# RWKV-7 scan on one Trainium2 core: 64x64 products that change partition halves by a table, and PSUM banks by kind

## The reference

```python
def wkv7_scan(r, w, k, v, a, b, reverse):
    def step(S, inp):
        rt, wt, kt, vt, at, bt = inp
        sa = jnp.einsum('bhvk,bhk->bhv', S, at)
        S = S * wt[:, :, None, :] + sa[..., None] * bt[:, :, None, :] + vt[..., None] * kt[:, :, None, :]
        return S, jnp.einsum('bhvk,bhk->bhv', S, rt)
    _, y = lax.scan(step, jnp.zeros((Bn, H, N, N), jnp.float32), xs, reverse=reverse)
```

## Time and profile before

| | |
|---|---|
| median of 3 runs (lowest to highest) | 2111.11 us (2107.66 to 2114.34) |
| the profiled execution | 2115.72 us, of which 2113.9 us from the first to the last instruction |
| the scan's first product to its last | 680.7 to 1156.7 us, 476 us |
| PE, PEld busy over the span | 83%, 65% |
| DVE, ACT, POOL busy over the span | 52%, 40%, 13% |
| mean granted PE clock | 0.92 of full |

### The profile page before, as it was taken

One profiled execution on the slowest core, in us unless ns is written; L12 is line 12 of the kernel. 1 busy time (PEld: TensorE's weight loads), 2 busy tenths in 40 slices (PEclk: granted clock), 3 DMA queues, 4 the chain that ended last, 5 costly groups with the idle time before them and its releaser, 6 DMA issues. The chain is left out here.

```text
span 2113.9 us, 48310 instructions
## 1 busy us (share of the span) xinstructions
PE 1755.0 (83%) x20423; PEld 1365.2 (65%) x20423; DVE 1109.5 (52%) x1786; ACT 846.8 (40%) x1228; POOL 280.2 (13%) x371
## 2 busy tenths in 40 slices
PE   3999999759776898898988399229999999999980
PEld 3777777647354888888887277226766666666650
DVE  4458988154575333333323832435656656556546
ACT  4246665110142333333322221025655556556532
POOL 0010000000110423333222200040000000000003
PEclk6999999969798999999999599559999999999995
DMA  5124444042101111110140211628999899899836
GB/s 186 31 80 143 144 144 120 23 177 80 59 0 56 53 54 54 54 54 29 54 177 33 83 65 65 246 81 323 362 366 382 350 366 380 351 367 378 352 156 249
DMA packets 95699, 355.54 MB, mean 168 GB/s; under 512 B 8984, under 2 KB 52295, under 8 KB 80936
## 3 DMA queue, kind: packets, MB, share of 16 engines
q1 hardware_dynamic: 82344, 306.83, 38.5%
q0 software_dynamic: 8576, 29.37, 3.7%
q10 hardware_dynamic: 4608, 16.78, 1.9%
HBM read 294.72 MB, written 56.13 MB: 166 GB/s over the span
## 5 line engine op out<-in xcount | busy, mean ns | idle before, releaser
L2191 DVE TENSOR_TENSOR e_rl<-proj,e_rh 128x1024 fp32r<-128x1024 f32 x256 | 304.9, 1223 | 148.6 <-ACT e_rh L2132 147.2
L2132 ACT ACTIVATE e_rh<-proj 128x1024 fp32r<-128x1024 f32 x256 | 258.7, 1054 | 82.2 <-PEq L1839 50.8
L51 PE MATMUL e_ph<-e_rh,e_xh 128*128 128x512 f32 x512 | 221.2, 432 | 15.9 <-DVE e_rl L2191 13.3
L2118 PE MATMUL e_py<-mix,proj 128*128 128x512 f32 x512 | 225.0, 592 | 0.7 <-issue 0.7
L51 PE MATMUL e_ph<-e_rh,e_xl 128*128 128x512 f32 x512 | 201.7, 394 | 0.0
L51 PE MATMUL e_ph<-e_rl,e_xh 128*128 128x512 f32 x512 | 200.2, 391 | 0.0
L51 PE MATMUL a_b<-a_xh,a_wh 128*128 128x512 f32 x432 | 176.8, 409 | 3.7 <-DVE a_wl L523 3.7
L51 PE MATMUL a_b<-a_xh,a_wl 128*128 128x512 f32 x432 | 169.4, 392 | 0.0
L51 PE MATMUL a_b<-a_xl,a_wh 128*128 128x512 f32 x432 | 169.3, 392 | 0.0
L2118 PEld LDWEIGHTS e_py<-mix,proj 128*128 128x128 f32 x512 | 97.1, 190 | 110.6 <-issue 108.0
L1499 ACT ACTIVATE s_th<-s_thb 128x512 f32<-128x512 f32 x128 | 76.5, 598 | 184.6 <-PE s_thb L1368 184.6
(11 more groups left out here) (349 smaller groups left out, 3262.9 us busy)
## 6 DMA issues: line engine op xcount, KB each, us to landing
proj<-in_moe_w SPq DMA_DIRECT2D x64, 2048.0 KB, 14.9
mix<-in_moe_w SPq DMA_DIRECT2D x32, 2048.0 KB, 9.0
proj<-scan_operands SPq DMA_DIRECT2D x64, 320.0 KB, 3.9
scan_operands<-f_late SPq DMA_DIRECT2D x64, 256.0 KB, 2.6
expert_rows<-e_yo ACTq DMA_DIRECT2D x32, 512.0 KB, 11.8
proj<-in_w_in SPq DMA_DIRECT2D x27, 512.0 KB, 4.1
proj<-in_x SPq DMA_DIRECT2D x16, 512.0 KB, 3.5
expert_rows<-proj SPq DMA_DIRECT2D x1, 7680.0 KB, 25.5
```

What stands on the lines that cost most here:

```text
L51: m = e.matmul(out, lhs[a], rhs[b], start=first and n == 0, stop=last and n == 2)
L2118: m = e.matmul(py[h][:, :], at[:, k, :], w2[j][:, k, h * HALF:(h + 1) * HALF], start=(k == 0), stop=(k == KF - 1))
L2132: e.activation(rh[s % RING][:, :], piece(j, s), ACT.Copy).then_inc(high, 1)
L2191: e.tensor_tensor(rl[s % RING][:, :], piece(j, s), rh[s % RING][:, :].bitcast(F32), ALU.subtract).then_inc(low, 1)
```

## The change

Each unit gets, for each level, a side by the table `SIDES`: with side 0 a product's output lies in the half that it was read from, with side 1 in the other half. Within `t` and `x` of a level half of the units cross and half do not, from level 2 on, and `h` crosses where the side changes from one level to the next; at level 1 all `x` and `t`, and half of the `h`, stay on the diagonal. `level_order` makes from the table the order of the products (one of the straight kind, one of the crossing kind, by turns) and the place of each. Products of the two kinds go to different banks: the two banks of a g, so far one for `x` and one for `t` and `h`, are now one tensor `s_lv` of two banks, by kind, and `x`, `t` and `h` of a g use both, one after the other. The first `x` of a step therefore waits for the copy of the last step's inverse (`hf_kept`).

In the pieces, direction 1 is kept in the other half (`c ^ d`), so that `inverse_applied`, `outputs_by_v`, `outputs_by_u` and `a_k_v` run over four quarters, and the shared banks are sorted by direction instead of by head or g. `products` of direction 1 with `OP_B` is cut into two of 64 columns each, since its two results now lie in different halves: 20 products instead of 16 for each g. `outputs_by_state` is cut into two parts, with `products(front, 1)` between them and a wait (`half_out`) ahead of the second. `states` stays on two quarters; its DVE part is one instruction instead of two. On ACT the copy of level 1 is two instructions (384 and 128 elements) and the copy into `s_ir` is four (128 elements each) instead of one of 512. POOL and SP are not touched.

The core of the diff, with "..." where lines are left out:

```diff
+SIDES = ((), (0, 0, 0, 0), (0, 0, 1, 1), (0, 1, 1, 0), (1, 1, 0, 0), (0, 1, 1, 0), (0, 0, 0, 0))
+def level_order(l):
+    now, then = SIDES[l], SIDES[l + 1]
+    kinds = {"x": [now[u] for u in range(HU)], "t": [now[u] for u in range(HU)], "h": [int(now[u] != then[u]) for u in range(HU)]}
...
-        xb = [ps(f"s_x{k}", [P, HALF]) for k in range(GP)]
-        thb = [ps(f"s_thb{k}", [P, HALF]) for k in range(GP)]
+        lv = [ps(f"s_lv{k}", [P, 2, HALF]) for k in range(GP)]
...
-                        for u, (h, d) in enumerate(units):
-                            for c in hs:
-                                i = mm(pub[g][c, u, :], hf[c, g, u, :], rec[j][c, g, h, d, 0:2 * CH], start=True, stop=True)
-                        i.then_inc(pu_full, 1)
+                        for h in range(2):
+                            for d in range(2):
+                                for c in range(2):
+                                    i = mm(pub[d][hs[c ^ d], 2 * g + h, :], hf[hs[c], g, last_at[2 * h + d], :],
+                                           rec[j][hs[c], g, h, d, 0:2 * CH], start=True, stop=True)
+                                if g == GP - 1 and h == 1:
+                                    i.then_inc(pu_full, 1)
...
-                    for d in range(2):
-                        for k, s in ((0, OP_B), (1, OP_K)):
-                            for h, c in quarters:
-                                i = mm(gb[h][hs[c], d, k, :], op[j][hs[h], g, d, s, hs[c]],
-                                       op[j][hs[h], g, d, OP_R:OP_A + 1, hs[c]], start=True, stop=True)
+                    for k, s in ((0, OP_B), (1, OP_K)):
+                        for h, c in quarters:
+                            i = mm(gb[h][hs[c], 0, k, :], op[j][hs[h], g, 0, s, hs[c]],
+                                   op[j][hs[h], g, 0, OP_R:OP_A + 1, hs[c]], start=True, stop=True)
+                    for h, c in quarters:
+                        mm(gb[h][hs[1 - c], 1, 1, :], op[j][hs[h], g, 1, OP_K, hs[c]],
+                           op[j][hs[h], g, 1, OP_R:OP_A + 1, hs[c]], start=True, stop=True)
+                    for k, s in ((0, OP_R), (1, OP_A)):
+                        for h, c in quarters:
+                            i = mm(gb[h][hs[c ^ (1 - k)], 1, 0, k * CH:(k + 1) * CH], op[j][hs[h], g, 1, OP_B, hs[c]],
+                                   op[j][hs[h], g, 1, s, hs[c]], start=True, stop=True)
...
-                        q6 = fill[6]
-                        fill[6] = lambda: (products(front, 1, back), q6())
...
+                            fill[6] = lambda: (outputs_by_state(back, 0), products(front, 1, back), outputs_by_state(back, 1))
...
-                            for u in range(HU):
-                                for c in hs:
-                                    i = mm(xs[g][c, u, :], al[c, l - 1, g * HU + u, :],
-                                           t1[c, g * HU + u, :] if first else th[c, g, u, 0, :], start=True, stop=True)
+                            elif n:
+                                e.wait_ge(hf_kept, (n - 1) * 2 + (g + 1))
+                            for _, u in xs:
+                                bank_of, slot_of = place["x", u]
+                                for c in range(2):
+                                    i = mm(lvu[g][hs[c ^ SIDES[l][u]], bank_of, slot_of, :], al[hs[c], l - 1, g * HU + u, :],
+                                           t1[hs[c], g * HU + u, :] if first else th[hs[c], g, before["t", u], :],
+                                           start=True, stop=True)
...
-                    e.activation(ir[j][:, :, :, 1, :].rearrange("p c e t -> p e c t"),
-                                 op[j][:, :, :, OP_R, :].rearrange("p g d (c t) -> p (g d) c t", c=2), ACT.Copy
-                                 ).then_inc(op_free, 1)
+                    for c in range(2):
+                        for d in range(2):
+                            i = e.activation(to_r(c ^ d, d), of_r(d, c), ACT.Copy)
+                    i.then_inc(op_free, 1)
```

More of the change, by code:

```diff
@@ L1088, with alternate @@
 HU = 4
+SIDES = ((), (0, 0, 0, 0), (0, 0, 1, 1), (0, 1, 1, 0), (1, 1, 0, 0), (0, 1, 1, 0), (0, 0, 0, 0))
+def level_order(l):
+    now, then = SIDES[l], SIDES[l + 1]
+    kinds = {"x": [now[u] for u in range(HU)], "t": [now[u] for u in range(HU)], "h": [int(now[u] != then[u]) for u in range(HU)]}
+    if l == LEVELS - 1:
+        del kinds["t"]
+    count, place = [0, 0], {}
+    for k in ("t", "h"):
+        for u in range(HU):
+            if k in kinds:
+                bank = kinds[k][u]
+                place[k, u] = (bank, count[bank])
+                count[bank] += 1
+    x_count = [0, 0]
+    for u in range(HU):
+        bank = kinds["x"][u]
+        place["x", u] = (bank, x_count[bank])
+        x_count[bank] += 1
+    def alternate(items):
+        two = [[i for i in items if place[i][0] == b] for b in range(2)]
+        out = []
+        while two[0] or two[1]:
+            out += [q.pop(0) for q in two if q]
+        return out
+    xs, ts = alternate([("x", u) for u in range(HU)]), alternate([(k, u) for k in ("t", "h") if k in kinds for u in range(HU)])
+    at = lambda n, key: place[key][0] * n[0] + place[key][1]
+    return xs, ts, place, tuple(x_count), tuple(count), {key: at(x_count if key[0] == "x" else count, key) for key in place}
 def rwkv_scan(nc, A, S, sem):
@@ L1204, in _ @@
                 mm = e.matmul
+                last_at = [order[LEVELS - 1][5]["h", u] for u in range(HU)]
                 def inverse_applied(m):
@@ L1286, in outputs_by_state @@
                                        start=False, stop=True, skip_group_check=True)
-                    i.then_inc(y_full, 1)
+                    i.then_inc((half_out, y_full)[part], 1)
                 def products(f, g, back):
@@ L1349, in step @@
                         first, last = l == 1, l == LEVELS - 1
+                        xs, ts, place, _, _, at = order[l]
+                        before = None if first else order[l - 1][5]
                         e.wait_ge(al_ready, n * (LEVELS - 1) + l)
```

176 lines of the change are left out of this document (104 added, 72 removed).

## The result

The changed kernel takes 2114.74 us (median of 20 runs, 2107.34 to 2118.91), the kernel before, timed beside it, 2109.78 us (20 runs, 2103.39 to 2119.19). The ratio is 1.0025, 95% interval [1.0016, 1.0035]: a quarter of a per cent slower, some 5 us, and not faster. The time lies inside the range of the prediction (2045 to 2125), 20 us above its forecast, with the sign against it.

What follows compares the result with a forecast made beforehand. The prediction took the supply of PE's code in 256-instruction blocks as the bound; gains of 13.0 (13 steps), 1.1 (step 0), 1.0 (clearing step) and 1.0 (end), together 16 us, made 2111.1 into 2095; range 2045 to 2125.

Steps and rivals of the forecast that it cites:

- The bound: In a scan step, PE's code arrives in blocks of 256 instructions, one about every 3.8 us, and PE uses them faster.
- PE's work: In a scan step, PE's MATMUL time falls by 7.8 us, from 24.5 to 16.7, through products on four quarters.
- The number of blocks: In a scan step, 32 added instructions raise 7.29 blocks to 7.41, costing 0.5 us a step.
- The price of a block: In a scan step, a block falls from 3.95 us to 3.75, so a step takes 27.8 us, 1.0 less.
- The first step: Step 0 of the scan: 5.4 blocks of 3.75 us, 20.3 us for 21.4, a gain of 1.1.
- The end: The end of the scan, 31 us, with chains over four engines uncovered: a gain of 1.0 us.
- The clearing step: The scan step with the clearing transfer, 37.0 us before: a gain of 1.0 us, the transfer's own price stays.
- Covered waits and the other engines: In a step, 3 us of uncovered waits hide under the supply, and ACT (10.7 us), DVE and POOL stay below 27.8: nothing.
- Rivals 1 and 2: Rival 1: supply doesn't bind, 1973 us, chance 0.12. Rival 2: blocks at down to 3.4 us, 2057, chance 0.14.
- Rival 3, the clock: In the scan, PE's standstills halve its clock: 2138 us; chance 0.12 for 2118 and more, 0.14 for 2106 to 2118.
- no gap would be as long as those of rows 7: Against a falling clock: no PE standstill as long as the 2.92 and 3.61 us beside another transfer before.
- Rival 4: Crossing products don't run beside straight ones: supply's pace plus 0.13 block, 2111 us; part of the no-gain case, no own chance.

Runs made afterwards that it cites:

- the split alone: The kernel before with only the 128-column products of direction 1 with OP_B cut in two, 32 more PE instructions a step, still two quarters: 1.0042.
- the quarters alone: The changed kernel with those products left 128 columns wide, so 1865 instructions a step as before, partly computing from the wrong half: 0.9996.

## Why the prediction was wrong, point by point

**The bound: right.** PE's code arrives in blocks of 256 instructions, in both kernels, and a step is as long as its blocks. One block more costs 3.5 us a step, and 6.6 us less of PE's work bring nothing.

**PE's work: nearly right.** Forecast 24.5 us a step before and 16.7 after; the traces have 24.6 and 18.0. With the other gaps of 1.4 us that is 19.4, where the prediction had 19.7 for work and waits together. The waits of 3 us were over-counted, the work under-counted.

**The number of blocks: right.** 7.29 and 7.41 were forecast from 1865 and 1898 instructions; the trace has 1865 and 1897.

**The price of a block: the step that failed.** "What a block costs after" read the 3.95 us that a block costs before as 3.75 for all and more for "the block with L1214", which takes longer than the supply, and let that excess vanish with the change. The block does hold more work than the supply, 4.54 us (serial loads, kernel before). But what sets its time in both kernels is another thing: the operand loads begin beside it and make its code 1.8 us late, 5.5 us for 3.7, and the change doesn't touch them. Before, that delay hid the block's long work; after, the work is short and the delay is still there. The term of 1.0 us a step, 13 of the 16 us of the sum, should have been: the other 6.4 blocks come 0.07 us sooner, 0.5 us less; 0.13 block more, 0.5 us; the late block, 5.52 before and 5.48 after. Their sum is about nothing, and measured is +0.1 us a step. The price of 3.75 itself was good: with the loads out of the way the mean is 3.70, and the step 27.5, even below the 27.8 of the forecast. A sign of it was at hand. The eight stretches of the earlier trace rows give 3.86 on the mean, the step 3.95, and the difference, 7.3 x 0.09 = 0.7 us a step, stood in no row. The earlier trace rows show the loads as the only other traffic, and the earlier trace rows a block that a transfer held up for much longer.

**The first step: right** (20.3 forecast and measured; 21.4 with the split alone, 20.0 with the quarters alone). **The end: right.** From the first `x` of step 15 to the scan's last product it is 29.9 us for 30.9, 1.0 less as forecast. **The clearing step:** "the transfer's own price stays", less 1.0; it took 2.4 us more. Of the four blocks that meet the loads and the transfer there, the kernel before had one whose code was not late, with three late ones, and the changed kernel had four late:

```profile
1060.28:1064.77 4.49, 4.49 (x127) 4.49 (x128) 0.85 (x2) 1.79 (x3) 0.45 (x1) 1.00 0.79 214
...
1059.01:1065.87 6.86, 2.96 (x129) 2.82 (x129) 0.42 (x1) 1.75 (x4) 0.00 (x0) 0.88 0.90 301
```

In the other kernels with the transfer in one piece the step lies between 33.9 and 40.0 us with no order that I could find, so whether the change or chance decides how many blocks are late is open.

**Covered waits and the other engines: right.** No wait for ACT, DVE or POOL took the place of the supply; ACT has 9.8 us of work a step where 10.7 was forecast.

**Rivals 1 and 2 fell.** No step of 20 us; no pace of 3.4: with PE asking for more at every boundary, the mean stays at 3.7.

**Rival 3, the clock,** came in a small part. Before, the granted clock was full in steps 1 to 12; after, nine blocks of these steps hold a good part of seven stretches at the lower level, 3.4 us each. Five of the seven begin within 0.7 us of the end of a gap of 2.2 to 3.0 us; but the longest gap of these steps, the one up to 775.96, was followed by the full clock. Two of the places:

```profile
736.00:739.80 3.80, 2.85 (x97) 2.66 (x97) 1.82 (x5) 1.68 (x5) 3.52 (x3) 0.58 0.05 11
...
803.00:807.00 4.00, 2.52 (x66) 2.52 (x70) 0.00 (x0) 0.82 (x3) 0.00 (x0) 0.73 0.14 47
```

The granted clock stands at 0.58 and 0.73 there, so at 1.2 GHz instead of 2.4 for a part. It costs little: these nine blocks take 3.9 us, some 0.2 more than the 3.7 of the undisturbed, because the stop at their end shrinks to 0.03 to 0.2 us in seven of them. That is about 2 us over the scan by this reckoning; no run tests it, and with the quarters alone the clock fell as often, in eight stretches, and the loss was gone. The prediction's "no gap would be as long as those of rows 7" was wrong, for the late block's stop is (3.60 us for the 3.61 there).

**Rival 4's number** (2111: the supply's pace and 0.13 block more) came nearest, 4 us off, but not by its mechanism: crossing products do overlap, at 15 ns.

That the loss belongs to the 32 instructions is shown (1.0042 with them alone, 0.9996 without them). What the clearing step and the clock add or take stays below what single profiles can tell.

## What to carry to other kernels

Before PE's work is cut, cut the trace at PE's restarts over a whole step: if its stretches hold the same number of instructions and last the same whatever is in them, a faster product was worth nothing here, and only fewer instructions, or their sooner arrival, can help; fewer that bring more work with them did not (1.0028). Compare the mean of such stretches with the length of a whole step; what is missing is in a stretch that was not looked at, here the one beside a burst of transfers. Large loads that stood together beside the code cost less when each waited for the one before, 0.4% in the kernel before and 0.8% in the changed one; there was time for it.

## What the runs showed of the hardware

- With four transfers of 320 KB at once, one interval between blocks of code a step is 5.5 us instead of 3.7, in either kernel; issued one behind another they leave 2 intervals over 4.5 us in 11 steps instead of 11 in the changed kernel, 1 instead of 10 in the one before. What sets the 3.7 us themselves no run here shows.
- 32 instructions on two quarters of the array take 0.93 us, so 128 MATMULs 3.7 us, which is just the pace at which their code comes. A stream of small products on two quarters and the supply were in balance; with the tails of matmuls counted, PE looked 91% busy and its work looked like the bound.
- A float32 transpose of 128x128 costs 112 ns for each of its two MATMULs, where a quarter of it costs 15 ns in a stream over four quarters: over seven times as much for four times the elements.
